# Early modulation with the weight matrix as the stationary operand, and one more late chunk of it on TensorE

## The reference, cut to what matters

```
silu_c = silu([c, c_ctx])                     # 2 x 1024, two streams: latent, context
mod    = silu_c @ w_mod[i] + b_mod[i]         # 2 x 6144: sh1 sc1 ga1 sh2 sc2 ga2
h  = rmsnorm(x) * (1 + sc1) + sh1;  x = x + ga1 * mixer(h)
h  = rmsnorm(x) * (1 + sc2) + sh2;  x = x + ga2 * peer_ffn(h)
out = rmsnorm(x_latent, final_g)
```

## Time and profile before

| what | us |
|---|---|
| median of 3 runs | 3805.61 (3804.53 to 3806.03) |
| the profiled execution | 3802.85 |
| its span, first to last instruction | 3801.1 |
| PE busy | 3287.8 (86%) |
| DVE busy | 2754.6 (72%) |
| ACT busy | 1635.6 (43%) |
| POOL busy | 1502.1 (40%) |
| mean granted TensorE clock | 0.974 of 2.4 GHz |
| HBM read | 1458.5 MB, 384 GB/s over the span |

### The profile page before, as it was taken

How to read it: one execution, slowest core, us unless ns; L and a number is a source line. 1 busy time by engine, 2 the same in 40 slices (tenths; PEclk the granted TensorE clock), 3 DMA queues, 4 the chain that set the end, 5 groups by cost and what they waited for, 6 DMA issues and landing times. The chain is left out here.

```text
span 3801.1 us, 37144 instructions
## 1 busy us (share of the span) xinstructions
PE 3287.8 (86%) x9600; PEld 1646.8 (43%) x9600; DVE 2754.6 (72%) x6377; ACT 1635.6 (43%) x4797; POOL 1502.1 (40%) x1329
## 2 busy tenths in 40 slices
PE   8888888889898988999998888898788888888887
PEld 4333333334444443455554456644334333333332
DVE  7877677778898888566665567677877767767765
ACT  3244444445555544533333325534444444444443
POOL 1144444444444444445444410044444444444442
PEclk9999999999999999999999989999999999999999
DMA  9499999999999999999999981199999999999997
GB/s 393 173 419 410 419 420 412 419 419 402 419 399 393 418 419 419 399 420 418 420 414 420 416 309 42 64 403 419 420 420 408 419 420 414 405 420 417 415 412 329
DMA packets 204053, 1463.08 MB, mean 385 GB/s; under 512 B 23224, under 2 KB 23736, under 8 KB 28480
## 3 DMA queue, kind: packets, MB, share of 16 engines
q0 software_dynamic: 190784, 1378.99, 88.3%
q1 hardware_dynamic: 13056, 81.71, 5.3%
HBM read 1458.52 MB, written 2.10 MB: 384 GB/s over the span
## 5 line engine op out<-in xcount | busy, mean ns | idle before, releaser
L1839 PE MATMUL ps<-arena 128*128 128x512 f32 x4888 | 2341.3, 618 | 448.5 <-ACT arena L1887 444.3
L2039 POOL DMA_INDIRECT arena<-experts,arena x1280 | 1477.8, 1155 | 2022.4 <-PE ps L1839 1616.0
L1920 DVE CUSTOM_DVE_ANT_0 arena<-arena 128x1024 f32<-128x1024 f32 x1280 | 1557.7, 1224 | 775.7 <-DMA arena<-experts,arena 756.5
L1839 PEld LDWEIGHTS ps<-arena 128*128 128x128 f32 x4888 | 895.5, 194 | 1702.5 <-ACT arena L1887 876.8
L1876 ACT ACTIVATE arena<-arena 128x1 f32<-128x1 f32 x1280 | 258.1, 202 | 1585.7 <-DVE arena L1920 1575.1
L1887 ACT ACTIVATE arena<-arena 128x128 f32<-128x128 f32 x1222 | 490.7, 402 | 91.6 <-PE ps L1839 5.5
L1880 ACT ACTIVATE arena<-arena 128x1 f32<-128x1 f32 x1280 | 377.0, 295 | 91.8 <-issue 4.9
L1548 PE MATMUL ps<-arena 128*128 128x256 f32 x1280 | 289.5, 379 | 1.1 <-ACT arena L1701 1.1
L1548 PEld LDWEIGHTS ps<-arena 128*128 128x128 f32 x1280 | 241.8, 190 | 60.4 <-issue 30.1
L923 PE MATMUL ps<-arena 128*128 128x256 f32 x1024 | 236.2, 385 | 4.5 <-PEq L2045 4.5
L923 PEld LDWEIGHTS ps<-arena 128*128 128x128 f32 x1024 | 198.2, 194 | 59.5 <-issue 34.8
(11 more groups left out here) (222 smaller groups left out, 2097.9 us busy)
## 6 DMA issues: line engine op xcount, KB each, us to landing
arena<-experts,arena POOLq DMA_INDIRECT x1280
arena<-diff_w_in SPq DMA_DIRECT2D x20, 1024.0 KB, 8.3
arena<-w_late POOLq DMA_DIRECT2D x16, 1024.0 KB, 5.4
arena<-w_mod SPq DMA_DIRECT2D x14, 1024.0 KB, 10.3
arena<-peer_wq SPq DMA_DIRECT2D x12, 1024.0 KB, 16.5
arena<-w_mod SPq DMA_DIRECT2D x4, 2048.0 KB, 17.8
arena<-w_early SPq DMA_DIRECT2D x8, 1024.0 KB, 9.5
arena<-b_mod POOLq DMA_DIRECT2D x12, 512.0 KB, 17.1
```

Of the source, the lines that this page charges most:

```text
L1839: last = nc.tensor.matmul(acc(t)[:, half * 512:(half + 1) * 512], diag[:, placed(n) % DIAGS, :], ring[:, slot_of(n), D + half * 512:D + (h ...
L1920: nc.vector.tensor_tensor_reduce(out=u_row, in0=u_row, in1=h_of(t), scale=1.0, scalar=0.0, op0=ALU.mult, op1=ALU.add, accum_out=dots[:, j: ...
L2039: nc.gpsimd.indirect_dma_start(out=ring[:, slot_of(n), :], out_offset=None, in_=experts, in_offset=bass.IndirectOffsetOnAxis(ap=idx_sb[:, ...
```

## The change

- `columns` on TensorE takes each 128 x 128 block of an early chunk as weights and streams the two columns of `silu_c`, 8 steps a block, straight into `f_cols_ps`. `product`, the row copies on ACT, the turning, DVE's half of chunk 3 and `pick` go. `m0_product` now counts finished chunks of columns, and the coefficients wait for the fourth.
- x pair 2 is loaded before chunks 2 and 3.
- Each bias is loaded once, for stream 0, and `late_out` adds it for both streams, stream 1 first.
- Late chunk j = 5 (`WHOLE`, halves 8 and 9) is a second product in `late_product`, from two buffers of its own, loaded by POOL after the folds. ACT copies two rows. Spreads 4 and 5 wait for both. DVE's two sums for it go.

```diff
@@ late streams, buffers, accumulators
-F_LATE_ROW_AT = 28392
+F_LATE_ROW_AT = (28392, 15360)
-F_LATE_W_AT = (29672, 31720, 18152, 34536)
+F_LATE_W_AT = (29672, 31720, 18152, 34536, 40680, 50920)
-F_LATE_ACC_AT = (53200, 13312, 26344)
+F_LATE_ACC_AT = (53200, 13312)
+    PE_HALVES, WHOLE = (8, 9), 5
...
-        return q % 3 if q < 2 * (LATE - 3) else q % 2 if q < 2 * (LATE - 2) else 3
+        return 4 + q % 2 if q in PE_HALVES else q % 3 if q < 2 * (LATE - 3) else q % 2 if q < 2 * (LATE - 2) else 3
...
-            return max([v + 1 for v in range(q) if late_buffer(v) == late_buffer(q)], default=0)
+            return max([v + 1 - 2 * (v > PE_HALVES[1]) for v in range(q) if late_buffer(v) == late_buffer(q)], default=0)
@@ late_tables
-            for s in range(late_streams(i)):
-                place = (at((F_GA1_AT if i == 0 else A_GA1_AT) + s * D, D) if kind == 2
-                         else mod_row(MOD2_AT, kind % 3, s))
-                eng.dma_start(place, b_mod[i:i + 1, kind * D:(kind + 1) * D].to_broadcast([P, D])
-                              ).then_inc(sem(n + "bias"), 16)
+            place = at(F_GA1_AT if i == 0 else A_GA1_AT, D) if kind == 2 else mod_row(MOD2_AT, kind % 3, 0)
+            eng.dma_start(place, b_mod[i:i + 1, kind * D:(kind + 1) * D].to_broadcast([P, D])
+                          ).then_inc(sem(n + "bias"), 16)
@@ late_spread
-        if i == 0 and j == PE_CHUNK:
-            pe.wait_ge(sem("m0_late_row"), 1)
+        if i == 0 and j in (PE_CHUNK, WHOLE):
+            pe.wait_ge(sem("m0_late_row"), 2)
@@ late_out
-            dve.wait_ge(sem(n + "bias"), 16 * (1 + 4 * late_streams(i)))
+            dve.wait_ge(sem(n + "bias"), 16 * 5)
-        for s in range(late_streams(i)):
-            last = nc.vector.tensor_tensor(late_place(i, ch, s), late_place(i, ch, s), late_bank(i, j, s), ALU.add)
+        for s in reversed(range(late_streams(i))):
+            last = nc.vector.tensor_tensor(late_place(i, ch, s), late_place(i, ch, 0), late_bank(i, j, s), ALU.add)
@@ fourier_sp
+        tiles_in(2)
         weights_in(2)
         weights_in(3)
-        tiles_in(2)
...
-        late_load(sp, 0, 3, 2 * (LATE - 3))
+        late_load(sp, 0, 3, PE_HALVES[0])
@@ fourier_pool
+        pool.wait_ge(sem("f_fold"), 2)
+        late_load(pool, 0, PE_HALVES[0], PE_HALVES[1] + 1)
@@ fourier_act
-            for ch in range(EARLY // 2) if lo == 0 else range(EARLY // 2, EARLY):
-                act.wait_ge(sem("m0_product"), ch + 1)
-                nc.scalar.copy(f_row(ch), bank(6 + ch % 2)[0:2, :]).then_inc(sem("m0_row"), 1)
@@ late_row_out
-        nc.scalar.copy(f_late_row, bank(4)[0:2, :]).then_inc(sem("m0_late_row"), 1)
+        nc.scalar.copy(f_late_row(0), bank(4)[0:2, :]).then_inc(sem("m0_late_row"), 1)
+        act.wait_ge(sem("m0_late_product"), 2)
+        nc.scalar.copy(f_late_row(1), bank(5)[0:2, :]).then_inc(sem("m0_late_row"), 1)
@@ fourier_dve
-        dve.wait_ge(sem(f"mod_w{EARLY - 1}"), 16)
-        for k in range(KD // 2, KD):
...
-        last.then_inc(sem("m0_part"), 1)
         norm(LT, NT)
         late_sum(dve, 0, 0)
         dve.wait_ge(sem("f_cols_in"), 16)
-        dve.wait_ge(sem("m0_cols"), 1)
+        dve.wait_ge(sem("m0_product"), EARLY)
...
-        late_sum(dve, 0, 8)
-        late_sum(dve, 0, 9)
@@ fourier_pe
-        def product(ch):
...
         def columns(ch):
-            pe.wait_ge(sem("m0_row"), ch + 1)
+            pe.wait_ge(sem(f"mod_w{ch}"), 16)
             for b in range(4):
                 o = 2 * (4 * ch + b)
...
+                for k in range(KD):
+                    last = nc.tensor.matmul(f_cols_ps[:, o:o + 2], f_weights(ch)[:, k, b * P:(b + 1) * P],
+                                            silu_c[:, k, :], start=(k == 0), stop=(k == KD - 1))
+            last.then_inc(sem("m0_product"), 1)
@@ late_product
+        last.then_inc(sem("m0_late_product"), 1)
+        for q in PE_HALVES:
+            pe.wait_ge(*late_landed(0, q))
+        for k in range(KD):
+            last = nc.tensor.matmul(bank(5)[0:2, :], silu_c[:, k, :], late_weights(0, PE_HALVES[k // 4])[:, k % 4, :],
+                                    start=(k == 0), stop=(k == KD - 1))
         last.then_inc(sem("m0_late_product"), 1)
@@ first_layer, gpsimd
-                    pool.wait_ge(sem("m0_late_used"), 2 * (LATE - 3) - 1)
+                    pool.wait_ge(sem("m0_late_used"), 2 * (LATE - 4))
```

More of the change, by code:

```diff
@@ L47 @@
 F_GAIN_AT = 12288
-F_ROW_AT = 13312
 F_AB_AT = 54736
@@ L74 @@
 F_W64_AT = 49896
-F_LATE_ACC_AT = (53200, 13312, 26344)
-F_PART_AT = 54224
+F_LATE_ACC_AT = (53200, 13312)
 F_EVEN_AT = (54224, 54736)
@@ L164, in build @@
     norms = pers[:, 112:208]
-    pick = pers[:, 96:100]
     subg = pers[:, 100:101]
@@ L223, in late_buffer_free @@
         if i == 0:
-            return max([v + 1 for v in range(q) if late_buffer(v) == late_buffer(q)], default=0)
+            return max([v + 1 - 2 * (v > PE_HALVES[1]) for v in range(q) if late_buffer(v) == late_buffer(q)], default=0)
         return q - 1 if q >= 2 * (IN_STEPS + 2) else q - 3
     def late_acc(i, j, s):
-        return at((F_LATE_ACC_AT[2 if j == 5 else j % 2] if i == 0 else LATE_A1_AT + 512 * (j % 2)) + 512 * s, 512)
+        return at((F_LATE_ACC_AT[j % 2] if i == 0 else LATE_A1_AT + 512 * (j % 2)) + 512 * s, 512)
     def late_ones(i):
@@ L260, in late_sum @@
         dve.wait_ge(*late_landed(i, q))
-        if q % 2 == 0 and (i or j != 5):
+        if q % 2 == 0:
             wait(dve, n + "spread", j - 1)
@@ L308, in late_spread @@
         n = f"m{i}_late_"
-        if i == 0 and j == PE_CHUNK:
-            pe.wait_ge(sem("m0_late_row"), 1)
+        if i == 0 and j in (PE_CHUNK, WHOLE):
+            pe.wait_ge(sem("m0_late_row"), 2)
         else:
-            pe.wait_ge(sem(n + "sum"), j + (0 if i == 0 and j > PE_CHUNK else 1))
+            pe.wait_ge(sem(n + "sum"), j - (1 if i == 0 and j > WHOLE else -1))
         wait(pe, n + "read", j if i else (0, 1, 2, 0, 3, 4, 5, 7)[j])
         for s in range(late_streams(i)):
-            if i == 0 and j == PE_CHUNK:
-                last = nc.tensor.matmul(late_bank(i, j, s), f_ident[0:2, s:s + 1].to_broadcast([2, P]), f_late_row,
+            if i == 0 and j in (PE_CHUNK, WHOLE):
+                last = nc.tensor.matmul(late_bank(i, j, s), f_ident[0:2, s:s + 1].to_broadcast([2, P]), f_late_row(j - PE_CHUNK),
                                         start=True, stop=True)
@@ L351, in build @@
     ITEMS = [(0, 0), (0, 1), None, (1, 0), (2, 0), (1, 1), (2, 1)]
-    f_late_row = at(F_LATE_ROW_AT, 512)[0:2, :]
     SPECIAL = {0: 0, 2: 32}
@@ L359, in build, with f_late_row @@
     f_cols_ps = bank(3, 32)
+    def f_late_row(r):
+        return at(F_LATE_ROW_AT[r], 512)[0:2, :]
     def f_weights(ch):
         return at(F_WMOD_AT + 4096 * ch, KD, 512)
[L364 to L369, removed]
     def f_ab(g):
@@ L539, in fourier_dve @@
         nc.vector.memset(late_ones(0), 1.0)
[L540 to L543, removed]
         def norm(lo, hi):
@@ L663, in fourier_pe, with columns @@
     def fourier_pe(pe):
-        def product(ch):
+        def columns(ch):
             pe.wait_ge(sem(f"mod_w{ch}"), 16)
[L666 to L673, removed]
-            pe.wait_ge(sem("m0_row"), ch + 1)
             for b in range(4):
                 o = 2 * (4 * ch + b)
[L677 to L686, removed]
+                for k in range(KD):
+                    last = nc.tensor.matmul(f_cols_ps[:, o:o + 2], f_weights(ch)[:, k, b * P:(b + 1) * P],
+                                            silu_c[:, k, :], start=(k == 0), stop=(k == KD - 1))
+            last.then_inc(sem("m0_product"), 1)
         def token_transform(g):
@@ L723, in fourier_pe @@
         pe.wait_ge(sem("silu"), 1)
-        product(0)
-        product(1)
+        for ch in range(EARLY):
+            columns(ch)
         pe.wait_ge(sem("e0_tables"), 32)
[L727 to L732, removed]
         pe.wait_ge(sem("dft_in"), 48)
```

## The result

The changed kernel takes **3827.8 us** (median of 4 runs, 3826.93 to 3828.94) against 3805.07: a ratio of 1.006, 95% interval 1.0042 to 1.0077, so +22.7 us, with an interval of some 16 to 29 us. The forecast was 3826.8. The profiled execution took 3828.07 us.

A forecast was written before the change was run, and what follows sets the result against it. PE's program order sets the front, and its delay moves the DMA-bound gathers one for one. Terms 21.4 + 1.2 - 1.4 = +21.2 us on the 3805.61 us median give 3826.8 us, range 3818 to 3836, chance 0.84.

The forecast's parts named there:

- The early phase (+21.4): Early modulation on PE: 256 pairs at 1.2 GHz, 0.215 us each, end at 64.0 us instead of 42.6, +21.4 us.
- the 0.43 us between later steps: First product on PE, earlier trace: steps start 0.85 us apart, later 0.43, so PE does not start at the upper clock.
- The transform's cold start (+1.2): Token transform after the early phase: starts at the lower clock, 3.7 us instead of 2.8, 0.3 more next group, +1.2 us.
- Nothing is credited: Earlier x load and single bias: 5 us of DMA and DVE's 0.73 us bias wait saved, counted as no gain.
- DMA waits between 43 and 103 us are the 0.73 us alone: PE and DVE before the second product: their only DMA wait is 0.73 us, said against the delay being partly taken up.
- Late chunk 5 (-1.4): Late modulation ahead of the mirror item: second product and spreads on PE take 17.9 us instead of 19.4, -1.4 us.
- Both spreads at the upper clock: Spreads after the second late product on PE: eight steps of 0.43 us, 3.4 us in all.
- The clock rises on dense loads: Rival, early phase: busy PE reaches the upper clock, phase ends at 41.1 us, 3802 us in all; chance 0.06.
- Loads don't slow when cold: Rival, early phase: clock stays low, loads keep their speed, end at 41.1 us, transform cold, 3804 us; chance 0.05.
- Don't overlap: Rival, early phase: cold loads take 0.34 us each in turn, end at 96 us, +53, 3859 us; chance 0.02.
- Taken up by DMA: Rival, after the early phase: DMA, idle until 64 us, takes up part of the delay, +10, 3816 us; chance 0.03.
- what would show it: Trace signs: clock about 0.5 until 64 us, matmuls 0.21 us apart, eviction 67.5, mirror item 143.5, first gather near 170.

The follow-up runs named there:

- e5: Changed kernel with five streaming matmuls, results unused, ahead of the early columns so they start at the upper clock: +21.3 us against the kernel before.
- e7: Changed kernel with five streaming matmuls ahead of the early columns and one behind every fourth step, 32 in all: +30.8 us against the kernel before.
- e2: Kernel before with the standing early weights alone: load order unchanged, two biases, late chunk 5 still summed on DVE; +21.7 us (1.0058).
- e8: Kernel before with x pair 2 loaded ahead of chunks 2 and 3, nothing else: ratio 1.0000 (0.9991 to 1.0009).
- e3: Changed kernel with the spreads contracting over all 128 rows instead of two, added rows multiplied by zero: +21.3 us against the kernel before.
- e6: Changed kernel with five streaming matmuls ahead of the early columns and one behind every eighth step, 16 in all: +52.7 us against the kernel before.

## Why the prediction was right, and where it was not

**The early phase (+21.4).** Right in mechanism and size. The step that carried it was the reading of the earlier trace rows: a stretch can be full of weight loads and still lose the clock, and a 128-wide load's growing part doubles. Measured: 0.213 us a pair where I took 0.215, end at 63.6 for 64.0. e5 shows the fall on record, with 0.11 us a pair ahead of it and 0.21 behind, and e7 the same loads at the upper clock to the end. (One reading was loose: the 0.43 us between later steps is in the trace, but the second load of the earlier trace rows does not show it, as its own distance is 0.76.) The Trainium skill ("TensorE: Matmul & The Clock Gate", section "LDWEIGHTS (loading the stationary operand)") gives a load as its columns / 1.2 ns with no term for the clock, 107 ns for 128. The trace has them 213 ns apart, so for f32 at 1.2 GHz the measurement decides against it.

**The transform's cold start (+1.2).** The eviction moved by 22.1 us, of which the phase is 63.6 - 42.6 = 21.0. That leaves 1.1 us at the eviction, against 0.9 forecast for this group and 0.3 for the next. Right in size.

**"Nothing is credited" for x sooner and the bias.** Right here: DVE stood idle for 21.45 us behind its last norm and sum, and e2, without these parts, is level up to 125 us. e8 shows why it depends on the company: on the old early part x sooner makes the coefficients 2.5 us late. The sentence that DMA waits between 43 and 103 us are the 0.73 us alone was wrong, by DVE's 1.19 us for late weights at 57.33; no term of the sum used it.

**Late chunk 5 (-1.4).** As arithmetic against the kernel before it held for the start of the mirror item: 125.07 to 143.26 is 18.2 us where I had 17.9 and the old order took 19.4. As a statement of what this part brings it was wrong. I counted the 6.13 us wait for DVE as still there, but standing weights delay PE more than DVE, and e2 shows 2.46 us left of it. In this kernel the part costs 143.26 - 140.79 = 2.5 us up to the mirror item, and 1.7 more in it. The sum came out since I laid the terms along the path of the changed kernel; the share of each part can't be read off them. A reader who takes the term as a gain of this part has its sign wrong. "Both spreads at the upper clock" held, but what follows was missed.

**Missed: the mirror item at 1.2 GHz (+1.7).** No term had it. Front in the sum: +21.2; measured +22.5. The mirror's eight matmuls of 5.34 instead of 3.65 us are that difference and more; up to the mirror item it was +20.8, so the other terms were 0.4 too large and hid a part of it. e3 shows that the rows of the spreads are the cause: only 2 of 128 were active. That the median came within 1.0 us of the forecast is partly luck, since the interval of the difference is 13 us wide; the front, 1.3 us off, is what bears the account out.

**The rivals.** "The clock rises on dense loads" is out by the 0.213 us that lasts to 63.6 us, and by e5. "Loads don't slow when cold" is out by the 0.213 us. "Don't overlap" is out as well, since 333 ns loads start 213 ns apart. "Taken up by DMA" is out: front +22.5, end +22.7 in the medians. As for "what would show it": short matmuls 0.21 us apart, eviction near 67.5, mirror near 143.5, all seen. The first gather came at 172.1 for 170, of which 1.7 us are the mirror item. The granted clock "about 0.5 until 64 us" can't be seen in the profile of this kernel at all, since its record begins later.

## What to carry to other kernels

Before you make the large operand the stationary one to save row copies and transposes, ask what the array streams in between: here, weight loads with two columns behind them were at best even at 2.4 GHz (7.2 against 7.03 us a chunk), and in their company the clock fell to 1.2 GHz, where they cost double. Work taken off an engine pays only as far as that engine is late in the kernel as it will be, not as it was: recompute its wait after the other parts of the change. Where a profile prints a clock for the start of a span, check it against the spacing of equal matmuls. Where a fall of the clock moves from run to run, compare single traces only from a point behind it.

## What the runs showed of the hardware that was not expected

- Streaming matmuls with 2 active rows and 128-wide weights (the spreads, 8 in 3.69 us) did not hold the clock: 0.57 from 146 to 148 us in the changed kernel, and 5.08 to 5.34 us for the eight matmuls behind them in seven traces. With 128 rows, same columns and time, it stayed at 1.00 in e3, with 3.65 us behind them in four traces. Products with weights 2 columns wide and all 128 rows held it (14 us from 125 us on).
- Once down, the clock was not raised by 49 us of back-to-back pairs (e5, 12 to 61 us), nor by pairs with one streaming matmul (two instructions) for every sixteen of them (e6, down from 12 us to the end of the phase). With one for every eight it did not fall in the whole phase (e7).
- Two 128-wide f32 loads overlap: each lasts 0.333 us and the next starts after 0.213 (changed kernel); at the upper clock a load lasts 0.192 (e7), and the next starts after 0.112 (0.11 in e5's first 3 us).
- A change of shape between matmuls of different weights cost about 0.09 us each time (e7: 0.98 us for eight pairs that take 0.90, and 0.95 for a filler of 0.86).
